# One ScalarE table set named by hand instead of two, and a longer filler on TensorE, in a hybrid SSD, GLA and gated-DeltaNet block

## The reference, cut to what matters

```
hl = rms_norm(x, norm_mix) * (1 + sc1) + sh1
even layer: SSD heads and GLA heads in parallel, odd layer: gated DeltaNet (GDN) heads
x  = x + g1 * mixer(hl)
x  = x + g2 * (silu(h @ w1) * (h @ w3)) @ w2
```

## Time and profile before

| | us |
|---|---|
| median of 3 runs | 2048.31 |
| lowest and highest | 2045.07 and 2048.42 |
| the profiled execution | 2048.42 |
| its span, first to last instruction | 2046.6 |
| PE busy | 1970.7 (96%) |
| DVE busy | 714.5 (35%) |
| ACT busy | 529.5 (26%) |
| POOL busy | 93.1 (5%) |

### The profile page before, as it was taken

How to read it: one execution, slowest core, us unless ns; L and a number is a source line. 1 busy time by engine, 2 the same in 40 slices (tenths; PEclk the granted TensorE clock), 3 DMA queues, 4 the chain that set the end, 5 groups by cost and what they waited for, 6 DMA issues and landing times.

```text
span 2046.6 us, 28698 instructions
## 1 busy us (share of the span) xinstructions
PE 1970.7 (96%) x12112; PEld 1198.9 (59%) x12112; DVE 714.5 (35%) x1476; ACT 529.5 (26%) x1170; POOL 93.1 (5%) x94
## 2 busy tenths in 40 slices
PE   6999999999999999999999999998999998999997
PEld 2444677785654444444444474444776666888886
DVE  2541675105750010000000065555858767010001
ACT  3121325414530020000000042224355776110000
POOL 0000231000000000000000000001211110000000
PEclk9999999999999999999999999999989998999999
DMA  6433111233201212122212132211224101344442
GB/s 280 164 149 126 42 41 42 103 124 125 85 22 62 93 62 82 63 81 82 77 62 72 63 123 67 78 62 63 84 88 183 64 22 43 124 144 144 155 145 91
DMA packets 27997, 193.48 MB, mean 95 GB/s; under 512 B 3004, under 2 KB 4285, under 8 KB 5854
## 3 DMA queue, kind: packets, MB, share of 16 engines
q1 hardware_dynamic: 27826, 191.51, 25.6%
q10 hardware_dynamic: 44, 0.14, 0.0%
HBM read 190.59 MB, written 1.05 MB: 94 GB/s over the span
## 4 chain that ended last, share of the span: by engine, by line
PE 88%; DVE 6%; ACT 3%; issue 1%; DMA 1%; SPq 0%; POOL 0%; ACTq 0%; DVEq 0%; POOLq 0%
PE psum L716 88%; DVE ws_sb L2034 1%; ACT ws_sb L1536 1%; DVE gl_tmp_sb L2034 1%; ACT arena_sb L1536 1%; DVE ws_sb L2037 1%; DMA arena_sb<-w 1%; DVE hT_sb L2037 0%; DVE arena_sb L2043 0%; PE psum L1126 0%; DVE arena_sb L2034 0%; PE psum L975 0%; ACT wide_sb L1536 0%; DVE hT_sb L2034 0%; ACT const_sb L1536 0%
## 5 line engine op out<-in xcount | busy, mean ns | idle before, releaser
L716 PE MATMUL psum<-hT_sb,ring_sb 128*128 128x512 f32 (+2 forms) x2272 | 797.9, 512 | 1.1 <-ACT hT_sb L1536 1.1
L716 PEld LDWEIGHTS psum<-hT_sb,ring_sb 128*128 128x128 f32 (+1 forms) x2272 | 427.9, 189 | 363.2 <-issue 338.6
L716 PE MATMUL psum<-arena_sb,ring_sb 128*128 128x512 f32 (+1 forms) x1216 | 396.2, 487 | 4.2 <-DVE small_sb L2040 1.9
L716 PEld LDWEIGHTS psum<-arena_sb,ring_sb 128*128 128x128 f32 x1216 | 231.5, 191 | 166.2 <-issue 144.0
L1536 ACT ACTIVATE ws_sb<-psum 128x512 f32<-128x512 f32 (+4 forms) x240 | 127.5, 535 | 717.7 <-PE psum L716 707.2
L716 PE MATMUL psum<-ring_sb,hT_sb 128*128 128x256 f32 (+3 forms) x1248 | 240.6, 372 | 0.1
L716 PEld LDWEIGHTS psum<-ring_sb,hT_sb 128*128 128x128 f32 (+1 forms) x1248 | 194.1, 176 | 52.5 <-issue 20.8
L2034 DVE TENSOR_TENSOR arena_sb<-ws_sb,psum 128x512 f32<-128x512 f32 (+1 forms) x44 | 24.4, 554 | 415.1 <-PE psum L716 415.1
L2037 DVE SCALAR_TENSOR_TENSOR xT_sb<-psum,mod_sb,xT_sb 128x256 f32<-128x256 f32 x48 | 23.2, 483 | 387.6 <-PE psum L716 387.1
L2037 DVE SCALAR_TENSOR_TENSOR ws_sb<-ws_sb,cols_sb 128x512 f32<-128x512 f32 (+1 forms) x176 | 123.7, 703 | 6.3
L1536 ACT ACTIVATE wide_sb<-xT_sb 128x512 f32<-128x512 f32 (+1 forms) x40 | 21.8, 544 | 399.8 <-PE psum L716 295.0
(11 more groups left out here) (173 smaller groups left out, 1448.0 us busy)
## 6 DMA issues: line engine op xcount, KB each, us to landing
ring_sb<-w SPq DMA_DIRECT2D x146, 1024.0 KB, 4.8
hT_sb<-w SPq DMA_DIRECT2D x16, 1024.0 KB, 4.9
arena_sb<-w SPq DMA_DIRECT2D x8, 1024.0 KB, 18.9
ring_sb<-w SPq DMA_DIRECT2D x8, 768.0 KB, 4.1
xT_sb<-x SPq DMA_DIRECT2D x1, 2048.0 KB, 10.3
const_sb<-consts SPq DMA_DIRECT2D x1, 2048.0 KB, 9.4
y<-xT_sb SPq DMA_DIRECT2D x1, 1024.0 KB, 4.8
ring_sb<-w SPq DMA_DIRECT2D x2, 256.0 KB, 3.7
```

What stands on the lines that cost most here:

```text
L716: return nc.tensor.matmul(o, l, r, start=start, stop=stop)
```

## The change

```diff
-LOG_EXP, SILU = 6, 18
+LN_TABLES = 5
@@ gemm_and_norm
                 if tag != "fin":
-                    keep_clock(4)
+                    keep_clock(5)
@@ ACT, norm(tag)
-                if tag in ("mix1", "fin"):
-                    load_tables(LOG_EXP)
+                load_tables(LN_TABLES)
...
-                if tag != "mix1":
-                    load_tables(SILU)
@@ ACT, l2_scales(first)
-                if first == 0:
-                    load_tables(LOG_EXP)
...
-                if first == 0:
-                    load_tables(SILU)
```

## The result

The changed kernel took 2062.1 us (median of 4 runs, 2058.99 to 2064.07), the kernel before 2048.36 (4 runs, 2045.07 to 2049.03). The ratio is 1.0068, 95% interval 1.0054 to 1.0082. The forecast was 2062.5 in a range of 2055.5 to 2068.5. In a later session the same two gave 2063.20 against 2049.32, ratio 1.0070 (1.0053 to 1.0087). One execution of experiment 5, at 10615 us, is left out of its median and ratio; one of experiment 9, at 2079.84 us, is in.

A forecast was written before the change was run, and what follows sets the result against it. The prediction took PE as the bound, busy 1970.7 of 2046.6 us, with longer ACT counting only where PE or the last store waits. Terms summed to 14.5 on 2048.42, giving 2062.9, stated as 2062.5, range 2055.5 to 2068.5.

The forecast's parts named there:

- The price of a load: Any chain on ACT: each table load costs 1.29 us from start to next start, with no added drain.
- First norm: First norm: the load delays Exp, and DVE, until now held by small work of its own, starts later; +0.49 us.
- mix1: Second mixer norm: two shifts stand ahead of the next projection and nothing covers the load; +1.29 us.
- ffn1: Second feed-forward norm: the fifth filler sets the projection's start and hides the load; +0.86 us, with four fillers +0.3.
- fin: Last norm: DVE starts right behind Exp and the output waits for its products, nothing beside the load; +1.29 us.
- ffn0: First feed-forward norm: the load counts and the fifth filler is covered; +1.20 us.
- GLA: Start of the GLA stage: the load now begins behind ACT's wait for PE, whose chain has no slack; +1.29 us.
- a rival at 0.12: Clock falls more: new pauses, as at GLA's start, bring one or two more low stretches; 2066 to 2070 us, chance 0.12.
- GDN start and recurrence: GDN stage: +1.29 us at the start, where PE's next sum needs Exp's bank, and +0.3 in the recurrence.
- The end of GDN: End of the GDN stage: six loads in a chain, 7.74 us, less ACT's idle 0.71 and 0.53; +6.5 us.
- Hidden elsewhere: Softplus of dt, feed-forward Silu loads and explicit loads ahead of squares: covered by other work, nothing taken.
- l2 scales: l2 scales: the load delays Silu to 1407.46, still ahead of PE's transposes at 1407.89; 0, upper end 1.29 us.

The follow-up runs named there:

- experiment 5: Changed kernel with filler matmuls around its pause at the GLA stage's start, one block ahead and two behind; ratio to the kernel before 1.0055.
- experiment 9: Changed kernel with four blocks of filler in place of five at the norms; median 2062.97 us beside the changed kernel's 2063.20.
- experiment 4: Kernel before with four table loads in a row between Ln and Exp of the last norm; ratio 1.0027, +5.5 us.
- experiment 6: Kernel before without the two written loads at the GDN stage's start, and one load added ahead of the recurrence's last seven steps; ratio 1.0002, 2048.48 us.
- experiment 3: Kernel before with only the six table loads at the GDN stage's end written in; ratio 1.0026, +5.3 us.
- 8: Kernel before with fillers at three pauses: one block at GLA's start, four ahead of the last l2 sums, four ahead of the second quarter's off-diagonal matmuls; ratio 0.9997.
- 11: Kernel before with three filler blocks in place of four at the norms and one at GLA's start; 2045.80 us beside 2049.32, ratio 0.9986.
- experiment 1: Kernel before with five filler blocks in place of four at the second mixer norm and both feed-forward norms; ratio 1.0009.
- 7: Kernel before with four filler blocks ahead of the second quarter's off-diagonal matmuls in the GDN stage; ratio 0.9992.
- experiment 2: Kernel before with GLA's first table load behind its wait, and one more load ahead of the stage's last Ln; ratio 1.0017, +3.5 us.

## Why the forecast was right, and where it was not

*The price of a load.* Right: 1.27 to 1.30 us in every open chain, and 5.15 for four (experiment 4).

*The norms.* First norm, mix1, ffn1 and fin are right to 0.02. ffn0 came to 1.55 for 1.20. It was not the fifth filler, since four give the same 1.55; the shift follows the Exp by 0.28 more than before, in both kernels and in the changed kernel's second profile. DVE's first product is no later behind the Exp than before; what holds the shift back is open. With four fillers, where the forecast had +0.3 for ffn1, experiment 9 measured +0.36.

*GLA, forecast 1.29, measured 5.33 and 3.64: the failed step of the sum.* The load is about 1.3 of it. The rest is half clock, which the forecast kept as a rival at 0.12 ("the pause at the GLA start grows to 1.9 us") and priced at nothing in the sum. The stage, read in each profile, against its mean clock from 465 to 490 us:

| load behind the wait? | clock 465 to 490 | stage against before's first profile |
|---|---|---|
| no (before, first; experiments 4, 6) | 0.93 each | 0 |
| no (experiment 3) | 1.00 | -0.97 |
| no (8 and 11, one filler) | 1.00, 1.00 | -0.96, -0.96 |
| no (1, 7) | 0.86, 0.86 | 1.30, 1.31 |
| no (before, second) | 0.80 | 2.48 |
| yes (5, filled) | 1.00 | 0.38 |
| yes (2) | 0.86 | 2.06 |
| yes (changed, second; 9) | 0.80, 0.80 | 3.64, 3.57 |
| yes (changed, first) | 0.80, and 588 us | 5.33 |

At equal clock the load costs 1.35, 0.75 and 1.1 to 1.2 us (rows with 1.00, 0.86 and 0.80), near the forecast but for the middle one. The clock accounts for the rest. Whether the longer pause makes the half clock longer, or three executions of the changed code happened to draw a long one, rests on few draws: with the short pause and no filler the seven profiles have a clock of 1.00, 0.93 three times, 0.86 twice and 0.80; with the long one 0.86 and 0.80 three times. Experiment 2's timed +3.5 (1.4 to 5.5) leans to the first, but its lower end is close to the bare load.

The timed executions have a mean clock too, and it leans the same way; 0.001 of it is some 4 us at half clock. With the load alone behind its wait (experiment 2) it was 0.9851 over 10 executions, against 0.9866 for the kernel before in the same session; for the changed kernel 0.9845 over 6 against 0.9870; with its pause filled (experiment 5) 0.9873 over 4 against 0.9869. So the kernels with the unfilled pause spent some 6 to 10 us more at half clock, and the filled one none. These means don't tell in which stage: experiment 4, which leaves GLA alone, has 0.9850 too, with its four loads lengthening the end of the span, where TensorE has no more work and the clock is 0.5. So part of the changed kernel's excess may lie elsewhere; the longer pause as the cause is likely, not shown.

*GDN start and recurrence, forecast 1.59, measured -0.24 and 0.07.* The step that failed is "the next sum on PE needs the bank which that Exp empties": PE goes on in another bank, and ACT has over 1 us to spare in the recurrence (experiment 6). Both loads are hidden, though the stage's length moves with its half clock by more than they cost (below). The low end that the forecast gave the first of them, 0.6, was too high.

*The end of GDN, forecast 6.5, measured 5.87.* The forecast let the first two loads count in full less ACT's idle 0.71. But the copy behind them is not what counts; the next squares on ACT waited 1.25 us for DVE. What DVE waits for is the Exp. Before, its merge began at 1720.53, which is 1.43 behind the end of that Exp, since DVE was busy with another sum; now it begins 0.10 behind. So 2.58 - 1.33 = 1.25 of the two loads counts: the merge is 9.74 later, and the stage 8.48.

```profile
1718.89 0.21 ACT L1536 ACTIVATE small_sb<-small_sb 128x16 f32<-128x16 f32 x1
...
1720.53 1.67 DVE L2037 SCALAR_TENSOR_TENSOR hT_sb<-hT_sb,small_sb,arena_sb 128x128 f32<-128x128 f32 x6
```

```profile
1729.95 0.22 ACT L1536 ACTIVATE small_sb<-small_sb 128x16 f32<-128x16 f32 x1
...
1730.27 1.93 DVE L2027 SCALAR_TENSOR_TENSOR hT_sb<-hT_sb,small_sb,arena_sb 128x128 f32<-128x128 f32 x7 [1.28 <-ACT small_sb L1536]
```

With the other four, less the idle 0.53 that the forecast took off too: 1.25 + 4 x 1.29 - 0.53 = 5.88, measured 5.87.

*Hidden elsewhere.* Right: l2 scales 0.01, GLA's end (the merge started at 599.73, PE's transposes at 609.22, later by the stage's shift alone).

*The total.* GLA was 2.3 to 4.0 above its term, ffn0 0.35 above, GDN start and end 2.2 to 2.5 below theirs. The median came out 0.4 from the forecast because these cancel, and because the timed median lies 2.7 us below the first profiled execution (0.7 below the second). That nearness is luck; the price of a load, the norms and the places with slack at the l2 scales and GLA's end are not. The terms without half clock, with 1.3 for GLA and nothing for GDN's start, sum to 12.6 us, an estimate from the two profiles; the timed differences are 13.7 and 13.9, with intervals from 11 to 18, so the timed runs alone can't tell the half clock's part from nothing. The margin of 2 us for the spread between executions was needed: nothing in one profile tells that GLA alone varies by 3.5 us. Of the forecast's signs, PE's idle time grew by 10.3 us (8 to 20 allowed) and the mean clock moved by 0.001.

## What to carry to other kernels

A table load costs its 1.29 us only where its activation is the last thing waited for; before counting it, look at which bank the next matmul writes and at what the next engine waits for last, since at two places called chains here, GDN's start and the recurrence, it cost nothing. A pause that grows next to work bound by TensorE costs its own length and may come with more half clock behind it, so it should be priced as a term and not left to a rival. A filler there gave back 0.96 us and more in the profiles, which the timed runs neither contradict nor show by itself, while one in a stage bound by another engine bought clock and 0.6 us at most. And fillers should be just as long as the wait that they cover: the fourth block at ffn1 was 0.84 us for nothing.

## What the runs showed of the hardware

The same instructions in the same order drew half-clock stretches between none (clock 1.00) and 10.2 us of them (0.80 over 25 us) at the same pause of 0.63 us at GLA's start, in different executions. The recurrence varies more: over the fourteen profiles its half clock from 1600 to 1720 us lay between none (experiment 1) and 17 us (experiment 5), and its length from 1440 to 1718 us between 5.5 us shorter and 2.0 us longer than in before's first profile. The timed runs show the same: of the 17 executions of the kernel before in the last session, the three shortest, 2040.8 to 2043.0 us, are the three with a mean clock of 0.991, and the eight from 2049.7 us up have 0.985 to 0.987. And what a stretch costs hangs on who is the bound: raising the clock from 0.62 to 0.81 over 18 us of the GDN stage gave back 0.6 us, while from 0.80 to 1.00 over 25 us of GLA it was 3.45 us (2.48 against -0.97).
